# A mixture-of-experts stage on one core: slots beyond an expert's first 128 worked in blocks of 64, two matmul passes instead of three

## What is computed

```python
p_top, g_idx = lax.top_k(pg, 1)                 # one of 4 groups for each token
v2, i2 = lax.top_k(el_sel, TOP_K_IN_GROUP)      # two of the group's 8 experts
...
h = jax.nn.silu(xb @ w_gate[e]) * (xb @ w_up[e])   # 1024 -> 512
return h @ w_down[e]                               # 512 -> 1024
...
out = jnp.zeros((T + 1, D), jnp.float32).at[slot_tok].add(ys * slot_gate[:, None])[:T]
```

## Time and profile before

| what | value |
|---|---|
| runs | 2106.82 us median of 3 (2106.13 to 2109.68) |
| profiled execution, first to last instruction | 2107.0 us (no other time is recorded for it) |
| PE busy / weight loads / DVE / ACT / POOL | 95% / 81% / 63% / 55% / 40% |
| granted TensorE clock, mean | 0.976 of full |
| DMA over the expert stage | 294 GB/s mean |

### The profile page before, as it was taken

One profiled execution on the slowest core, in us unless ns is written; L12 is line 12 of the kernel. 1 busy time (PEld: TensorE's weight loads), 2 busy tenths in 40 slices (PEclk: granted clock), 3 DMA queues, 4 the chain that ended last, 5 costly groups with the idle time before them and its releaser, 6 DMA issues. The chain is left out here.

```text
span 2107.0 us, 39855 instructions
## 1 busy us (share of the span) xinstructions
PE 1993.2 (95%) x12627; PEld 1697.4 (81%) x12628; DVE 1323.6 (63%) x2411; ACT 1159.0 (55%) x2421; POOL 846.2 (40%) x1024
## 2 busy tenths in 40 slices
PE   7999999979999999989999689999999999999997
PEld 6888888867777787878788578888888888888886
DVE  5333333328888888845565568677777668695763
ACT  4211111128888889953333257666666657684662
POOL 3322222223656644431332345444444435444443
PEclk9999999989999999989999899999999999999998
DMA  7433333366363443224544579989999988998963
GB/s 227 136 120 120 122 121 120 112 171 165 105 166 105 126 114 91 69 70 154 168 158 140 204 242 357 355 276 307 302 283 318 339 266 277 361 347 271 310 200 88
DMA packets 320307, 420.62 MB, mean 200 GB/s; under 512 B 27289, under 2 KB 230681, under 8 KB 320192
## 3 DMA queue, kind: packets, MB, share of 16 engines
q1 hardware_dynamic: 290912, 351.34, 51.0%
q0 software_dynamic: 29296, 68.03, 12.5%
HBM read 344.35 MB, written 110.41 MB: 216 GB/s over the span
## 5 line engine op out<-in xcount | busy, mean ns | idle before, releaser
L742 ACT ACTIVATE prob<-score,nmax 128x512 f32<-128x512 f32 (+3 forms) x464 | 264.3, 579 | 24.9 <-DVE nmax L892 24.5
L60 PE MATMUL proj<-w_in_lo,n1T_hi 128*128 128x512 f32 (+1 forms) x640 | 244.1, 381 | 3.1 <-DVE w_in_lo L245 3.0
L62 PE MATMUL proj<-w_in_hi,n1T_hi 128*128 128x512 f32 (+1 forms) x640 | 239.5, 374 | 0.0
L61 PE MATMUL proj<-w_in_hi,n1T_lo 128*128 128x512 f32 (+1 forms) x640 | 239.4, 374 | 0.0
L892 DVE TENSOR_REDUCE nmax<-score 128x2 f32<-128x1024 f32 (+3 forms) x232 | 212.5, 919 | 41.5 <-PE score L940 39.8
L60 PE MATMUL u_ps<-wu_lo,xT_hi 128*128 128x256 f32 x752 | 216.3, 288 | 0.0
L61 PE MATMUL u_ps<-wu_hi,xT_lo 128*128 128x256 f32 x752 | 212.7, 283 | 0.0
L62 PE MATMUL u_ps<-wu_hi,xT_hi 128*128 128x256 f32 x752 | 212.6, 283 | 0.0
L1887 DVE TENSOR_TENSOR wg_lo<-raw_pieces,wg_hi 128x1024 fp32r<-128x1024 f32 x124 | 147.6, 1219 | 83.6 <-ACT wg_hi L1848 83.5
L807 POOL TENSOR_SCALAR prob<-prob,scale,lam 128x512 f32<-128x512 f32 (+3 forms) x168 | 137.7, 831 | 151.8 <-DVE scale L879 142.4
L264 DVE TENSOR_TENSOR cosx<-proj,rope_sb 128x512 f32<-128x512 f32 (+1 forms) x64 | 37.9, 592 | 219.3 <-PE proj L62 219.3
(11 more groups left out here) (261 smaller groups left out, 5210.4 us busy)
## 6 DMA issues: line engine op xcount, KB each, us to landing
raw_pieces<-in_w_down SPq DMA_DIRECT2D x64, 1024.0 KB, 12.0
raw_pieces<-in_w_gate SPq DMA_DIRECT2D x62, 1024.0 KB, 11.4
raw_pieces<-in_w_up SPq DMA_DIRECT2D x62, 1024.0 KB, 11.9
qk_scratch<-qkT SPq DMA_DIRECT2D x94, 256.0 KB, 2.6
xT_sb<-in_xT SPq DMA_DIRECT2D x16, 512.0 KB, 5.0
h<-in_x SPq DMA_DIRECT2D x16, 512.0 KB, 5.7
acc_scratch<-h SPq DMA_DIRECT2D x16, 512.0 KB, 3.0
n_scratch<-n SPq DMA_DIRECT2D x16, 512.0 KB, 4.9
```

The costliest lines, as they stand in the source:

```text
L60: pe.matmul(out, hi, w_lo, start=first, stop=False)
L61: pe.matmul(out, lo, w_hi, start=False, stop=False)
L62: return pe.matmul(out, hi, w_hi, start=False, stop=last)
L742: act.activation(prob[:, n % RING, c, 0:w], score[:, n % BUFS, c, 0:w], ACT.Exp, bias=nmax[:, c, n:n + 1], accum_out=part[:, c, n:n + 1]). ...
```

## The change

A slot beyond an expert's first 128 now goes to a list of 64 (`SLOT_BLOCKS` is 1 + 30 lists; rows 64 to 127 of the list's column hold it). For each expert the small blocks run first, then one full block of 128. For a small block the 64 rounded rows and their 64 remainder rows stand side by side as one 128-wide stationary operand, so two matmuls (against the rounded and the remainder weights) give all four partial products: the rounded rows' result in one half of the PSUM partitions, the remainder rows' in the other. ACT copies one half out, DVE adds the other. To have that operand, DVE packs the remainders of rows 64 to 127 behind the rounded ones after every `split_xT`.

Three orders change in the full block too: DVE's `normalize` moves from the block's first third to behind `split_xT`; ACT's `square` moves behind `highs(3, 4, 5)`; POOL's `store` moves behind the copy of `own`, next to `fetch_whole`. POOL reads two more counts from memory ahead of a full block. The table grows from 512 to 992 lists.

```diff
-SLOT_BLOCKS = SEQ // P
+HP = P // 2
+SLOT_BLOCKS = 1 + (SEQ - P) // HP
...
-                    dve.scalar_tensor_tensor(out=dest[:, t, :], in0=rank_block[:, :], scalar=1.0 - P * LISTED,
-                                             in1=place_to[:, :], op0=ALU.mult, op1=ALU.add).then_inc(place_step, 1)
+                    dve.tensor_scalar(block_step[:, :], rank_block[:, :], 1.0, float(E - HP * LISTED), ALU.max, ALU.mult)\
+                        .then_inc(place_step, 1)
+                    dve.wait_ge(place_step, base + 9)
+                    dve.tensor_tensor(dest[:, t, :], block_step[:, :], place_to[:, :], ALU.add).then_inc(place_step, 1)
...
-                    with eng.Fori(first, last) as b:
-                        one_block(b, e, False, e * SLOT_BLOCKS + b - first, e * SLOT_BLOCKS + b + 1 - first)
-                one_block(last, e, replaced, e * SLOT_BLOCKS + last - first, (e + 1) * SLOT_BLOCKS if replaced else 0)
+                    with eng.Fori(first, last) as n:
+                        small_block(n + e, e, n, last - n)
+                full_block(last + e, e, replaced)
...
                     add(b)
-                    scale(b)
-                    store(b)
+                    normal_root(b)
+                    aim_store(b)
                     move_on(b)
                     pool.tensor_copy(own[:, :].bitcast(I32), slots[:, bass.ds(within(here), 1), :].bitcast(I32))\
                         .then_inc(own_ready, 1)
+                    store(b)
                     fetch_whole(b)
...
+                    smalls = small_count(pool, e + 2) - small_count(pool, e + 1)
+                    one_block(b, e, smalls * N_EXPERTS + (e + 1))
...
+                def small_block(b, e, n, left):
+                    act.wait_ge(g_done, b + 1)
+                    act.wait_ge(h_turned, b * 2 + 1)
+                    act.wait_ge(y_ready, b + 1)
+                    act.copy(g_part[0:HP, :], g_ps[HP:P, :]).then_inc(part_out, 1)
+                    act.wait_ge(summed, n * 4 + 1)
+                    act.activation(hid[0:HP, :], hid[0:HP, :], ACT.Silu).then_inc(silu_ready, 1)
+                    copy_u_part(b, 0)
+                    copy_small_hT(b, 0)
+                    copy_u_part(b, 1)
+                    copy_xT(b + 1)
+                    copy_small_hT(b, 1)
+                    square(b)
...
-                    highs(0)
-                    square(b)
-                    highs(1, 2)
+                    highs(0, 1, 2)
...
                     highs(3, 4, 5)
+                    square(b)
                     copy_hT(b, 0)
...
+                    dve.wait_ge(xT_split, b + 1)
+                    dve.tensor_copy(xT_hi[:, :, P:], xT_lo[:, :, HP:]).then_inc(xT_packed, 1)
...
+                def small_block(b, e, n, left):
+                    dve.wait_ge(part_out, n * 3 + 1)
+                    dve.tensor_tensor(hid[0:HP, :], g_part[0:HP, :], g_ps[0:HP, :], ALU.add).then_inc(summed, 1)
+                    small_hidden(b, n, 0)
+                    split_small_hT(b, 0)
+                    small_hidden(b, n, 1)
+                    split_small_hT(b, 1)
+                    split_xT(b + 1)
+                    normalize(b)
+                    dve.wait_ge(y_done, b + 1)
+                    dve.tensor_copy(y_part[HP:P, :], y_ps[0:HP, :, :].rearrange("p a b -> p (a b)")).then_inc(summed, 1)
...
                     lows(0, 1, 2)
-                    normalize(b)
...
                     split_xT(b + 1)
+                    normalize(b)
                     lows(6, 7, 8, 9, 10, 11)
...
+                def packed_product(out, packed, w_hi, w_lo, first, last):
+
+                    pe.matmul(out, packed, w_lo, start=first, stop=False)
+                    return pe.matmul(out, packed, w_hi, start=False, stop=last)
...
+                    turn_h(b, 0)
+                    turn_x(b + 1)
+                    pe.wait_ge(y_ready, b + 1)
```

More of the change, by code:

```diff
@@ L1252, in block_table @@
                     dve.wait_ge(place_step, PLACED + 4)
-                    dve.tensor_copy(starts[0:1, :], start_row[:, :]).then_inc(place_step, 1)
-                    dve.tensor_scalar(end_row[:, :], start_row[:, 1:], -1.0, None, ALU.add).then_inc(place_step, 1)
-                    dve.wait_ge(place_step, PLACED + 6)
-                    dve.tensor_copy(ends[0:1, :], end_row[:, :])
+                    dve.tensor_copy(starts[0:1, :], start_row[:, :])
                 low_swa(0, 0)
@@ L1590, in load_pair, with experts @@
                   .rearrange("p (a b) -> p a b", a=(4, 8, 2)[j // 2]), source_pair(w_d, e, j)).then_inc(raw_in[j], 16)
-def experts(nc, sem, n2_d, acc_d, slots_d, empty_d, final_g, power, out, w_gate, w_up, w_down, ident, passed, wg, wu, starts, ends, hi_ready,
+def experts(nc, sem, n2_d, acc_d, slots_d, empty_d, final_g, power, out, w_gate, w_up, w_down, ident, passed, wg, wu, starts, hi_ready,
             lo_ready, raw, raw_in):
@@ L1774, in move_on, with one_block @@
                     pool.sem_inc(passed, 1)
-                def one_block(b, e, replaced, here, after):
+                def one_block(b, here, after):
                     pool.wait_ge(x_in, b * 16 + 16)
@@ L1791, in _ @@
                 pool.memset(y[:, :], 0.0).then_inc(y_ready, 1)
+                pool.memset(hid[:, :], 0.0).then_inc(h_turned, 1)
+                first_smalls = small_count(pool, 1)
                 pool.wait_ge(own_free, 32)
-                gather(0, 0)
+                gather(0, within(first_smalls * N_EXPERTS))
                 pool.memset(whole[:, :], 0.0).then_inc(at_ready, 1)
@@ L1840, in copy_hT, with copy_small_hT, copy_u_part, full_block @@
                         .then_inc(hT_ready, 1)
-                def one_block(b, e, replaced, here, after):
+                def copy_small_hT(b, half):
+                    act.wait_ge(h_turned, b * 2 + (half + 2))
+                    src = g_ps if half == 0 else u_ps[:, 0, :]
+                    act.copy(hT_hi[:, 2 * half:2 * half + 2, HP:P],
+                             src[:, 0:HALF].rearrange("p (k n) -> p k n", k=2)[:, :, 0:HP]).then_inc(hT_ready, 1)
+                def copy_u_part(b, half):
+                    act.wait_ge(u_done, b * 2 + (half + 1))
+                    act.copy(u_part[0:HP, half, :], u_ps[HP:P, half, 0:HALF]).then_inc(part_out, 1)
+                def small_block(b, e, n, left):
[11 more added lines that the diff above has]
+                    square(b)
+                    act.wait_ge(y_done, b + 1)
+                    act.wait_ge(own_ready, b + 2)
+                    act.activation(y[HP:P, :], y_ps[HP:P, :, :].rearrange("p a b -> p (a b)"), ACT.Copy,
+                                   scale=own[HP:P, 1:2]).then_inc(y_scaled, 1)
+                def full_block(b, e, replaced):
                     def highs(*ks):
@@ L1912, in hidden, with split_small_hT, small_hidden, small_block @@
                         .then_inc(hid_ready, 1)
[L1914 removed]
+                def split_small_hT(b, half):
+                    dve.wait_ge(hT_ready, b * 2 + (half + 1))
+                    src = g_ps if half == 0 else u_ps[:, 0, :]
+                    dve.tensor_tensor(hT_hi[:, 2 * half:2 * half + 2, 0:HP],
+                                      src[:, 0:HALF].rearrange("p (k n) -> p k n", k=2)[:, :, 0:HP],
+                                      hT_hi[:, 2 * half:2 * half + 2, HP:P], ALU.subtract).then_inc(hT_split, 1)
+                def small_hidden(b, n, half):
+                    cols = slice(half * HALF, (half + 1) * HALF)
+                    dve.wait_ge(part_out, n * 3 + (half + 2))
+                    dve.tensor_tensor(u_part[0:HP, half, :], u_part[0:HP, half, :], u_ps[0:HP, half, 0:HALF], ALU.add)\
+                        .then_inc(summed, 1)
+                    dve.wait_ge(silu_ready, b + 1)
+                    dve.wait_ge(summed, n * 4 + (half + 2))
+                    dve.tensor_tensor(hid[0:HP, cols], hid[0:HP, cols], u_part[0:HP, half, :], ALU.mult).then_inc(hid_ready, 1)
+                def small_block(b, e, n, left):
+                    dve.wait_ge(part_out, n * 3 + 1)
[8 more added lines that the diff above has]
+                    dve.tensor_copy(y_part[HP:P, :], y_ps[0:HP, :, :].rearrange("p a b -> p (a b)")).then_inc(summed, 1)
+                    dve.wait_ge(summed, n * 4 + 4)
+                    dve.wait_ge(y_scaled, n + 1)
+                    dve.scalar_tensor_tensor(out=y[HP:P, :], in0=y_part[HP:P, :], scalar=own[HP:P, 1:2], in1=y[HP:P, :],
+                                             op0=ALU.mult, op1=ALU.add).then_inc(y_ready, 1)
+                def full_block(b, e, replaced):
                     def lows(*ks):
```

109 lines of the change are left out of this document (74 added, 35 removed).

## The result

The changed kernel takes 2245.45 us, the median of 4 runs (2243.28 to 2254.42), where the kernel before took 2108.25 us in the same comparison: 1.066 times as long, 95% interval [1.0643, 1.0678]. The profiled execution has a span of 2242.5 us, 135.5 more than before's.

What follows compares the result with a forecast made beforehand. TensorE sets the pace at 18.0 us a block, weight DMA at 20.5 in rows of single-block experts. From 2107.0: -24 small blocks, +7 singles, +6.5 end, +2.0 start, -8.5 in all, gives 2099 us; 8-in-10 range 2074 to 2125.

Steps and rivals of the forecast that it cites:

- The gather starts 4.3 us after a block begins: POOL's gather of the next x, queued behind normalize and store, starts 6.6 us later than before; at most 5.3 into small blocks.
- the forecast's L: Landing time of the gathered x; a small block takes L + 9.4 us, and the forecast covers L from 6.2 to 7.5.
- I take 7.0 as the mean: Landing of the gather for small blocks: 7.0 us, between 7.3 to 8.1 beside streaming weights and 4.2 to 5.1 without.
- 0, at most 1 each: Loss in us of a pair's full block behind a small one, where little DMA was expected in flight.
- The slow rival: Gather lands later than in any row, at 8.1 us; small blocks take 17.5, singles lose 2 each: 2122 us, chance 0.29.
- The clock: Rival: PE's idle time lets small blocks' down stages fall to 1.2 GHz, 54 us on top: 2153 us, chance 0.03.
- The small block of 16.4 us: Small block's length with x there 11.3 us in, then turns and down stage; 1.6 saved each, 24 us for 15.
- Singles: Single blocks wait 1.2 us for x: four lone ones lose 5 us, rows 2 us since weights cover it; together +7.
- Without any wait 12.4 us: Length of a small block with two passes instead of three and no waiting; 5.6 us saved each, 84 for 15.
- The end, "+6.5": After the last block, packing, final, store and read-back delay the last gather and addition: 6.5 us lost, nothing covering it.
- The start, "+2.0": Loading the table of lists, grown from 768 KB to 1488 KB, delays the first list's reading by 2.0 us, at most 5.
- Packing: DVE's copy of 512 columns behind split_xT, taken as 0.68 us from the nearest row of that size.

Runs made afterwards that it cites:

- e11: Changed kernel without the pass against the remainders of the down weights in small blocks (8 matmuls less, behind the wait for x): 2230.12 us.
- e6: Changed kernel with normalize and square put back early in every block, POOL's order left as changed: 2107.39 us.
- e4: Changed kernel with dummy transposes on PE ahead of each wait for x (40 in a small block, 20 in a full one): 2200.42 us.
- e8: Changed kernel with its three orders put back, and a small block's normalize moved between second hidden product and second remainder of h: 2107.33 us.
- e10: Kernel before the change plus only the 192-column layout of xT_hi and the packing copy, which nobody reads: 2112.10 us, ratio 1.0008.
- e13: Changed kernel, old POOL order, normalize and square mid-block in full blocks, small-block normalize behind second hidden product, plus 128 unused SBUF bytes: 2092.39 us.

## Why the prediction was wrong

It said 2099 us; measured 2245. The kind of loss was foreseen: a gather issued late, and PE waiting for `x` at its turn. The sum was not: small blocks cost 65 us more than forecast (+40.9 instead of -24), full blocks of pairs 35 (+35.2 instead of 0), singles 49 (+56.0 instead of +7). Two signs that it had named for being wrong are seen, full blocks of pairs over 18.5 us and a granted clock below 1.00. By its own steps:

- **"The gather starts 4.3 us after a block begins" is the step that failed**, in what it is counted from more than in its size. Its instants came from a block whose `x` was in time: there `normalize` ends with the block. With `x` late, `split_xT` is late, `normalize` behind it, the store behind that, and the next gather too. The start measured 5.05 us in the small block above (4.7 to 6.4 in all 15, where "at most 5.3" was allowed), and in the full one 5.67 (1596.13 - 1590.46), for which nothing was charged. That it came out so near is luck: a late `x` puts off the block's end and the next gather alike, and e11, which shortens what is behind the wait, moves the start. The order of store and gather was seen; that it closes a ring through the gather's own landing was not. e6 shows that the place of `normalize` and `square` makes `x` late, e11 that the start isn't fixed to the block. What this cost is an estimate: with the forecast's L of 7.0 and the 12.1 us of e4, where the clock stayed up, a pair takes 2 x 19.1 = 38.2 us instead of 16.4 + 18.0, which is 57 us for 15 pairs.
- **"I take 7.0 as the mean" for the landing failed as well**, and as a size: 8.4 in the median, 7.7 at the least, above all in the full blocks of pairs, for which the 4.2 to 5.1 of quiet stretches stood and "0, at most 1 each". These stretches are quiet no more (1.05 MB of weights in the flight of 1596.13), and that is why these blocks wait: the full one of 2167.27 starts its gather 5.6 us after its beginning like the others, and with a landing of 5.2 it waits for nothing. The slow rival had a later landing; with its 19 us for each us of L, 8.4 would have made 2126. That is less than a fifth of the miss, because the formula counts L in 15 small blocks and 4 lone singles, and 44 blocks waited: 1.4 us in each is 62. What the prediction drew from the Trainium skill ("DMA: Bandwidth & Descriptors", Queues, rings and completion order), that a gather loses little to the weights, does not hold in this trace: 4.5 to 5.2 us without them, 7.7 to 9.2 beside them. Whether the DMA engines take turns packet by packet, as that section says, no run here shows.
- **The clock** had a chance of 0.03, because it stayed at 1.00 where PE stood "for 6 us in three blocks"; that is 2 us a block (PE's longest wait in that stage was 2.3 us). Here a small block has one piece of 4.4 us, and the clock halved. The size given, 54 us, was near the 45 of e4, in part by luck: it was worked out for small blocks alone, and the clock fell in 14 others too. The chance was the mistake. The warning of the Trainium skill's page "TensorE: Matmul & The Clock Gate" (HAM oscillation), that a wait for a DMA in each round of a loop lets the clock fall, was right here: 0.50 behind the wait at 1583.20.
- **Together**: the ring's 57 us (estimate), the landing's 62 and the clock's 45 are some 20 more than the 144 us between the forecast and the profiled span. The three overlap; in rows of singles, for one, 20.5 us a block were in the forecast already.
- **The small block of 16.4 us** is 20.99: 0.75 from the start, 1.68 from the landing (8.68), 2.16 from turns and down stage at the lower clock (7.26 instead of 5.1); together 4.59.
- **Singles**, "+1.2": the four lone ones lost 2.7 (20.86) to 5.1 us (23.23) against 18.14 before; in rows the weights did not cover it, 65.75 instead of 61.40.
- **"Without any wait 12.4 us"** was nearly reached: 13.32 in e8.
- **The end, "+6.5"**: right. The last addition starts 7.6 us behind the last matmul's end (2220.48 + 0.40), where it was 1.3. PE and DVE there:

```profile
2220.48 0.40 PE L62 MATMUL y_ps<-wd_hi,hT_hi 128*128 128x512 f32 x1
```

  and the addition:

```profile
2228.50 1.22 DVE L2021 TENSOR_TENSOR x<-x,y 128x1024 f32<-128x1024 f32 x1 [8.16 <-DMA x<-acc_scratch,own]
```

- **The start, "+2.0"**: right in its place: from the issue of the table's load to the reading of the first list it took 9.34 us instead of 6.93, 2.4 more, with 6.75 us of idle time instead of 4.80. The stage began 2.8 us earlier all the same: the table's load was issued 2.0 us earlier in this run (1204.84 against 1206.82), and the first gather landed in 5.0 us instead of 7.6. The row:

```profile
1214.18 0.18 POOL L1730 COPY fetch<-slots 128x1 int32 x1 [6.75 <-DMA own<-in_empty]
```

- **Packing**, 0.68, measured 0.43. It is hidden in e10; in the changed kernel it is a link of the ring.

Not settled: that the landing is late beside the weights is shown, by the last three gathers too, but not how the weights' transfers hold the gather's up; and which of `normalize` and `square` would close the ring alone.

## What to carry to other kernels

When a step is moved behind another one, follow its results until they come back to the thing it now waits for: if they do, the price is a period (here a landing plus some 13 us), and most of the time saved elsewhere in the block is handed back as waiting. A start measured from a block's beginning in a trace without the wait says nothing about the same block with it. Such a period costs nothing while it fits into the block's own work: with landings of 4.5 to 5.2 us it did, with 7.7 to 9.2 it did not. And a wait for a DMA on TensorE can cost more than itself, by the clock behind it.

## What was unexpected of the hardware

- The granted clock fell to 0.50 behind an idle piece of 4.38 us and stayed there for 5.20 us of full work. It fell also behind a wait of 1.98 us (1433.62), and in the last small block behind two of 1.2 and 1.4 us (2196.13); behind waits of 1.72 (1603.85) and 3.28 us (1907.39) the stage ran at 1.00.
- An indirect gather of 512 KB lands in 4.5 to 5.2 us when no weights are loaded, and in the changed kernel in 7.7 to 9.2 beside them. The DMA share does not tell the two apart: it was 0.81 in the flight of 2172.89, which landed in 5.2 us, and 0.82 in that of 1596.13, which took 7.7.
- Every kernel with small blocks has gate stages of 5.58 to 5.60 us in full blocks instead of 5.44 (medians), for the same 24 matmuls; e10 and e13 exclude this layout and this offset, and the cause is open.
